# Pitch 1280 bytes and separate start offsets for the streamed activations of a two-layer hybrid decoder trunk

## The reference, cut to what matters

```python
def swiglu_ffn(h, w_in, w_out):
    gate, up = jnp.split(h @ w_in, 2, axis=-1)
    return (jax.nn.silu(gate) * up) @ w_out

for i in range(DEPTH):                       # DEPTH = 2
    h = layer_norm(ALPHA * h + 0.5 * swiglu_ffn(h, ffn_w_in[i, 0], ffn_w_out[i, 0]), ...)
    mix = short_conv_mixer(h, ...) if i % 2 == 0 else gla_mixer(h, ...)
    h = layer_norm(ALPHA * h + mix, ...)
    h = layer_norm(ALPHA * h + 0.5 * swiglu_ffn(h, ffn_w_in[i, 1], ffn_w_out[i, 1]), ...)
return h[:, 16:]
```

## Time and profile before

| What | Value |
|---|---|
| Median of 3 runs | 1023.55 us (1022.95 to 1026.16) |
| Span of the profiled execution | 1020.9 us |
| PE busy | 1009.0 us, 99% of the span, 7866 matmuls |
| DVE, ACT, POOL busy | 71%, 50%, 12% |
| Matmuls with 272 columns of `x_hi`/`x_lo` in groups | 3552 |
| Matmuls with 272 columns of `mid_hi`/`mid_lo` in groups | 1386 |
| Mean DMA rate | 173 GB/s |

### The profile page before, as it was taken

How to read it: one execution, slowest core, us unless ns; L and a number is a source line. 1 busy time by engine, 2 the same in 40 slices (tenths; PEclk the granted TensorE clock), 3 DMA queues, 4 the chain that set the end, 5 groups by cost and what they waited for, 6 DMA issues and landing times.

```text
span 1020.9 us, 18997 instructions
## 1 busy us (share of the span) xinstructions
PE 1009.0 (99%) x7866; PEld 988.4 (97%) x7866; DVE 723.9 (71%) x1078; ACT 512.6 (50%) x746; POOL 122.1 (12%) x136
## 2 busy tenths in 40 slices
PE   9999999999999999999999999999999999999997
PEld 7999999999999999999999999999989999999885
DVE  5856557689889856567697555667897999666444
ACT  6534435464456544444565343444868675444430
POOL 2000003320002000003210000134243320000000
PEclk9999999999999999999999999999999999999999
DMA  9966555637752966556638665555355648865531
GB/s 255 264 189 182 165 169 172 185 99 207 227 167 83 260 174 182 162 168 179 178 115 244 179 175 161 170 162 142 101 137 170 193 117 244 228 194 189 169 122 41
DMA packets 324263, 176.58 MB, mean 173 GB/s; under 512 B 6658, under 2 KB 320048, under 8 KB 324176
## 3 DMA queue, kind: packets, MB, share of 16 engines
q1 hardware_dynamic: 323664, 174.15, 58.8%
q0 software_dynamic: 480, 1.15, 0.4%
q10 hardware_dynamic: 32, 0.07, 0.0%
HBM read 174.29 MB, written 1.05 MB: 172 GB/s over the span
## 4 chain that ended last, share of the span: by engine, by line
PE 92%; DVE 4%; ACT 1%; issue 1%; POOL 1%; POOLq 0%; DVEq 0%; ACTq 0%
PE bank L1295 23%; PE bank L1290 23%; PE bank L1293 23%; PE bank L1309 3%; PE bank L1311 3%; PE bank L1310 3%; PE bank L1453 2%; PE bank L1455 2%; PE bank L1454 2%; PE bank L1335 2%; PE bank L1334 2%; PE bank L1336 2%; DVE weights_lo L806 1%; DVE rms L1203 1%; DVE resid L922 0%
## 5 line engine op out<-in xcount | busy, mean ns | idle before, releaser
L448 ACT ACTIVATE weights_hi<-raw_weights 128x1024 fp32r<-128x1024 f32 x335 | 353.8, 1059 | 414.6 <-PE bank L1295 306.6
L806 DVE TENSOR_TENSOR weights_lo<-raw_weights,weights_hi 128x1024 fp32r<-128x1024 f32 x334 | 415.5, 1250 | 204.9 <-ACT weights_hi L448 203.6
L1290 PE MATMUL bank<-x_hi,weights_hi 128*128 128x272 f32 (+1 forms) x1584 | 227.6, 286 | 0.0
L1295 PE MATMUL bank<-x_lo,weights_hi 128*128 128x272 f32 (+1 forms) x1584 | 227.4, 285 | 0.0
L1293 PE MATMUL bank<-x_hi,weights_lo 128*128 128x272 f32 (+1 forms) x1584 | 225.0, 284 | 0.0
L1295 PEld LDWEIGHTS bank<-x_lo,weights_hi 128*128 128x128 f32 x1584 | 208.0, 188 | 0.0
L1290 PEld LDWEIGHTS bank<-x_hi,weights_hi 128*128 128x128 f32 x1584 | 207.4, 188 | 0.4
L1293 PEld LDWEIGHTS bank<-x_hi,weights_lo 128*128 128x128 f32 x1584 | 206.1, 188 | 0.0
L1290 PE MATMUL bank<-mid_hi,weights_hi 128*128 128x272 f32 x462 | 68.2, 288 | 0.0
L1293 PE MATMUL bank<-mid_hi,weights_lo 128*128 128x272 f32 x462 | 68.1, 288 | 0.0
L1295 PE MATMUL bank<-mid_lo,weights_hi 128*128 128x272 f32 x462 | 68.0, 288 | 0.0
(11 more groups left out here) (231 smaller groups left out, 1198.8 us busy)
## 6 DMA issues: line engine op xcount, KB each, us to landing
raw_weights<-in_ffn_w_in_dram SPq DMA_DIRECT2D x176, 512.0 KB, 4.1
raw_weights<-in_ffn_w_out_dram SPq DMA_DIRECT2D x70, 512.0 KB, 4.0
raw_weights<-in_conv_w_in_dram SPq DMA_DIRECT2D x24, 512.0 KB, 4.1
raw_weights<-in_gla_w_in_dram SPq DMA_DIRECT2D x24, 512.0 KB, 3.9
raw_weights<-in_ffn_w_out_dram SPq DMA_DIRECT2D x24, 384.0 KB, 3.5
raw_weights<-in_conv_w_out_dram SPq DMA_DIRECT2D x8, 512.0 KB, 4.6
raw_weights<-in_gla_w_out_dram SPq DMA_DIRECT2D x8, 512.0 KB, 4.7
x_tok<-in_x_dram SPq DMA_DIRECT2D x2, 512.0 KB, 4.9
```

Of the source, the lines that this page charges most:

```text
L448: nc.scalar.activation(w_hi[:, n % RING, :], raw[:, n % RAW, :], ACT.Copy).then_inc(hi_split, 1)
L806: nc.vector.tensor_tensor(w_lo[:, s, :], raw[:, n % RAW, :], w_hi[:, s, :].bitcast(F32), ALU.subtract).then_inc(lo_split, 1)
L1290: nc.tensor.matmul(ps, block_of(w_hi, n, k - k0), hi[:, k, cols], start=first and k == k0, stop=False)
L1295: mm = nc.tensor.matmul(ps, block_of(w_hi, n, k - k0), lo[:, k, cols], start=False, stop=last and k == k1 - 1)
```

## The change

No instruction is added, removed or moved: on every engine the built program has the same instructions in the same order. What changes is where tensors lie. `LINE` is 64 values, 256 bytes. Start addresses within 256 bytes, and pitches, worked out from the allocations of both programs:

| Tensor | Start mod 256, before | Pitch before | Start mod 256, after | Pitch after |
|---|---|---|---|---|
| weights_hi | 128 | 4096 (slot) | 128 | 4096 |
| weights_lo | 128 | 4096 (slot) | 0 | 4096 |
| x_hi | 128 | 1152 | 192 | 1280 |
| x_lo | 128 | 1280 | 64 | 1280 |
| mid_hi | 32 | 1088 | 160 | 1280 |
| mid_lo | 160 | 1088 | 96 | 1280 |
| yc_hi | 192 | 1088 | 224 | 1280 |
| yc_lo | 192 | 1088 | 32 | 1280 |
| zg_hi | 160 | 1096 | 96 | 1104 |
| zg_lo | 224 | 1096 | 224 | 1104 |
| y_hi, y_lo | 32, 32 | 1024 | 32, 32 | 1024 |

1152 is 4.5 times 256, so the blocks of `x_hi` began at 128 and 0 in turn; 1280 is 5 times 256, so after the change every block of a tensor begins at the same offset. 1088 moves by 64 from block to block, 1096 by 72, 1104 by 80. `scaled` is gone; `d_ref` is a tensor of its own in the attention's area, behind `gate_area`, inside the bytes that `mid_lo` has in the FFNs. In the convolution's area `yc_hi` and `yc_lo` now come ahead of `cu`, `u_sb` and `conv_t`.

```diff
+    LINE = 64
+    PITCH = -(-T // LINE) * LINE
...
         w_hi = sb("weights_hi", [P, RING, KU * P], F32R)
+        pad_lo = sb("pad_lo", [P, LINE // 2])
         w_lo = sb("weights_lo", [P, RING, KU * P], F32R)
-        x_hi = sb("x_hi", [P, KD, T + 16], F32R)[:, :, 0:T]
-        x_lo = sb("x_lo", [P, KD, T + 48], F32R)[:, :, 0:T]
+        pad_x = sb("pad_x", [P, 3 * LINE // 4])
+        x_hi = sb("x_hi", [P, KD, PITCH], F32R)[:, :, 0:T]
+        pad_x_lo = sb("pad_x_lo", [P, LINE // 2])
+        x_lo = sb("x_lo", [P, KD, PITCH], F32R)[:, :, 0:T]
...
-        scaled = sb("scaled", [P, 3, T])
...
-            mid_hi = inner.enter_context(nc.sbuf_tensor("mid_hi", [P, KF, T], F32R))
-            mid_lo = inner.enter_context(nc.sbuf_tensor("mid_lo", [P, KF, T], F32R))
+            inner.enter_context(nc.sbuf_tensor("pad_mid_hi", [P, LINE // 2], F32))
+            mid_hi = inner.enter_context(nc.sbuf_tensor("mid_hi", [P, KF, PITCH], F32R))[:, :, 0:T]
+            inner.enter_context(nc.sbuf_tensor("pad_mid_lo", [P, 3 * LINE // 4], F32))
+            mid_lo = inner.enter_context(nc.sbuf_tensor("mid_lo", [P, KF, PITCH], F32R))[:, :, 0:T]
...
+            conv.enter_context(nc.sbuf_tensor("pad_yc_hi", [P, 3 * LINE // 4], F32))
+            yc_hi = conv.enter_context(nc.sbuf_tensor("yc_hi", [P, KD, PITCH], F32R))[:, :, 0:T]
+            conv.enter_context(nc.sbuf_tensor("pad_yc_lo", [P, LINE // 4], F32))
+            yc_lo = conv.enter_context(nc.sbuf_tensor("yc_lo", [P, KD, PITCH], F32R))[:, :, 0:T]
...
-            yc_hi = conv.enter_context(nc.sbuf_tensor("yc_hi", [P, KD, T], F32R))
-            yc_lo = conv.enter_context(nc.sbuf_tensor("yc_lo", [P, KD, T], F32R))
...
-        d_ref = scaled
+        d_ref = gb("d_ref", [P, 3, T])
...
-            zg_hi = raw_stage.enter_context(nc.sbuf_tensor("zg_hi", [P, KD, T + 2], F32R))
-            zg_lo = raw_stage.enter_context(nc.sbuf_tensor("zg_lo", [P, KD, T + 2], F32R))
+            zg_hi = raw_stage.enter_context(nc.sbuf_tensor("zg_hi", [P, KD, T + 4], F32R))
+            zg_lo = raw_stage.enter_context(nc.sbuf_tensor("zg_lo", [P, KD, T + 4], F32R))
```

## The result

| | before | after |
|---|---|---|
| Median, us | 1023.31 (20 runs, 1022.72 to 1027.54) | 1025.95 (20 runs, 1024.91 to 1029.45) |
| Ratio to before | 1 | 1.0023, 95% interval 1.0013 to 1.0032 |
| Span of the profiled execution | 1020.9 | 1027.7 |

A forecast was written before the change was run, and what follows sets the result against it. PE, busy 99% of the span, was taken as the bound through time per matmul; terms +3.0, +1.0, -0.2, -0.2 and -0.3 summed to +3.3 us, a 1024.2 us span and 1026.9 us time, range 1009 to 1034 us.

The forecast's parts named there:

- the waits: On PE: stays 99% busy with the same few waits; a new wait would mean a shared address had made one.
- the 2.00 us for sixteen matmuls of x_hi: In the changed timeline, sixteen 272-column matmuls of x_hi should take 2.00 us instead of 1.98.
- x_hi, 272 columns: 2 x 1184 matmuls going from in-turn 123.75 ns to constant 125.0 ns: +3.0 us, bounds -9 and +15.
- x_hi, 256 columns: 2 x 400 matmuls going from 116.9 to 118.1 ns: +1.0 us.
- x_lo: Matmuls streaming x_lo, constant before and after, only the offset moves: 0, bounds -6 and +6 us.
- mid, yc, zg: Matmuls streaming these tensors become constant or nearly so: mid -0.2 us, yc -0.2 us, zg -0.3 us.
- The rings at 512 columns: 264 matmuls of 512 columns, weights_lo at 0, mid as stationary operand: 0, bounds +-0.6 us.
- d_ref and the small tensors: Instructions and waits as before; d_ref shares bytes with mid_lo but is written after its last read: 0.
- The rival of avoided collisions: Streams beginning where their weights begin collide with the load; avoiding this gives -3.9 us, 1019.7 us; chance 0.33.
- The rival of bad offsets: Constant offsets 64 bytes from the ring are bad; 126.25 ns for x and mid, 1033.9 us; chance 0.15.
- The rival of no change: Only the mean over offsets counts, so new patterns have the present mean: 1023.6 us; chance 0.12.
- the fast half everywhere: x_hi's fast half becomes the rule for all of x, mid, yc and zg: -26 us, 998 us.

The follow-up runs named there:

- both halves of the change: Before plus only the weights_lo, x_hi and x_lo lines: 1025.87 us, ratio 1.0016; before plus only all the other lines (mid, yc, zg, d_ref): 1023.89 us, ratio 0.9993.
- the sweep: Two kernels with x and mid at pitch 1280, both rings at 128, each tensor at a constant distance from 0 to 224: 1025.77 and 1029.46 us, one run each.

## Why the prediction was right

The sign, the size and the place (x_hi with 272 columns, then all 256-column groups) came out: +2.6 us against +3.3. Term by term it was less right than its sum, and the nearness of the sum is in part luck. Of its own signs, the waits and the 2.00 us for sixteen matmuls of x_hi came out, though as 1.01 and 0.99; x_lo takes 0.99 us instead of 1.00 and a unit with 256 columns 2.87 instead of 2.83. And what it named as the way to be wrong is what the runs show: the offset against the ring matters more than the step from block to block. The change did cost x_hi its good pattern, but not because a constant offset is worse than one in turn: at the constant distance of 192 x_hi is at 123.3 to 123.4 ns, and in turn it is at 125.0 and at 126.5 to 126.7 in the two kernels with pitch 1152 for all.

1. **x_hi, 272 columns:** +3.0 forecast, +2.6 in the traces. It was priced with one constant rate, 125.0, and the two products are at 126.0 and 123.7. Their mean is near 125.0 by chance. The step that failed is "a constant offset gives 125.0 whatever it is", taken from one value with 272 columns and from two agreeing ones with 256.
2. **x_hi, 256 columns:** +1.0 forecast, +1.9 measured, 119.3 instead of 118.1: mis-sized for the same reason, the new distances 128 and 0.
3. **x_lo:** 0 forecast, -1.6 with 272 columns and +0.7 with 256, inside the bounds of 6.
4. **mid, yc, zg:** -0.7 forecast, -1.4 measured, half of it mid, whose gain needs both halves of the change.
5. **The rings at 512 columns:** 0 forecast, +0.4 measured.
6. **d_ref and the small tensors:** nothing, as forecast; waits and chain are the old ones.

The rival of avoided collisions saw something real and had it half right: x_lo, moved off its weights' offset, gained 1.3 ns (2.5 had been put on it), and with 256 columns x_hi on weights_lo and x_lo, moved onto it, lost 2.3 and 1.6. But x_hi on weights_hi, moved off to 64, lost 1.8 instead of gaining. The distance matters, but zero is not its worst value: by the sweep 64 and 128 are worse and 192 is best. The argument against it in the prediction, that the excess grows with the columns and so can't come from the weights' load, doesn't hold: the runs show that the weights' address alone changes the rate. The rival of bad offsets was right on one product in three of x with 272 columns (126.0 ns against the 126.25 it had named). The rival of no change, that the mean over offsets is all that counts, is out: one common distance takes all groups of x with 272 columns to 123.3 to 123.4 ns. The gain that lay open, 12.9 us, is over three times the 3.9 us of the collision case; the prediction's price of "the fast half everywhere" was 26 us, and half of that was near it.

## What to carry to other kernels

Where PE is busy 99% of the span and the rate of a matmul is above its columns over the clock, look at the start addresses of stream and weights: the distance between the two, modulo 256 bytes here, was worth up to 3 ns of 125 and 6 of 119 per matmul. Take a pitch that keeps the distance the same for every block, give all tensors the same distance to all weights, and try several such common distances in the kernel itself: mixed neighbours cost, so a sweep with mixed distances tells only roughly what a common one gives (only 192 and 160 were tried as common ones here), and the alternating ones weren't foreseen by any theory. Don't give each tensor an offset of its own: that was this change, and it made several rates out of what could be one. Compare traces behind the start.

## What the runs showed of the hardware

- The distance of the moving operand's start from the weights' start, modulo 256 bytes, changes the rate of these float32r matmuls: 123.3 to 126.7 ns with 272 columns, 113.3 to 119.6 with 256. A shift of everything by 64 bytes changed no rate of x, mid, yc or y by more than 0.1 ns, a shift of the weights alone changed one by 2.9 ns.
- What streamed before carries over: the first matmuls of a group differ from the later ones (121, 134, 125 and 122 ns in the first four of x_lo before, 124 to 127 in the next three), and a whole group can run at another rate behind another predecessor (x_lo with 256 columns at distance 0: 119.5 ns in three kernels behind a group at 0, 117.7 and 117.8 in two behind a group at 192 or 128). With alternating distances x_hi was at 123.8 and 125.0 ns at identical addresses in two kernels, one execution each.
- The start of a run can stay at half rate some microseconds longer, 11 matmuls against 21 between 10 and 12.5 us, while the row's granted clock says 1.00 both times. It was worth 4.65 us between two profiled executions, more than the change; comparing the spans of the two profiles gives 6.8 us where the medians differ by 2.6.
- Open: whether the two reads collide, and where; why 192 is best; why what streamed before carries over; and which rate an alternation settles to. Constant distances between multiples of 32 bytes were not tried.
